# MLP up units: one 512-column matmul for both parts of the activations, and conditioning sums once a layer

## The reference

```python
def sq_relu_mlp(h, w1, w2):                      # w1 1024 x 4096, w2 4096 x 1024, once in each of two layers
    return jnp.square(jax.nn.relu(h @ w1)) @ w2
...
mod = jax.nn.silu(c) @ w_ada + b_ada             # w_ada 1024 x 3072: shift, scale, gate of the last block
shift, scale, gate = jnp.split(mod, 3, axis=-1)
```

## Time and profile before

| | us |
|---|---|
| median of 3 runs | 997.27 |
| lowest, highest | 995.95, 998.62 |
| the profiled execution | 995.88 |
| its span | 994.0 |

### The profile page before, as it was taken

How to read it: one execution, slowest core, us unless ns; L and a number is a source line. 1 busy time by engine, 2 the same in 40 slices (tenths; PEclk the granted TensorE clock), 3 DMA queues, 4 the chain that set the end, 5 groups by cost and what they waited for, 6 DMA issues and landing times. The chain is left out here.

```text
span 994.0 us, 14517 instructions
## 1 busy us (share of the span) xinstructions
PE 971.0 (98%) x6042; PEld 876.7 (88%) x6042; DVE 647.8 (65%) x843; ACT 507.0 (51%) x624; POOL 14.0 (1%) x12
## 2 busy tenths in 40 slices
PE   6999999999999999999999999998999999999997
PEld 5998888889999988988889999987999999988885
DVE  5889936676666668866676766658434777646473
ACT  6734464564434447555664444447344555445533
POOL 0000000000000000000000000000000000002000
PEclk9999999999999999999999999999999999999999
DMA  9834426466777764634466777765655545456611
GB/s 316 302 128 129 169 85 211 149 213 212 242 242 224 249 216 131 209 128 127 149 212 213 258 233 233 248 176 172 229 194 186 170 135 163 170 182 241 197 58 43
DMA packets 122853, 187.37 MB, mean 188 GB/s; under 512 B 5315, under 2 KB 88740, under 8 KB 122788
## 3 DMA queue, kind: packets, MB, share of 16 engines
q1 hardware_dynamic: 122628, 186.17, 56.8%
q10 hardware_dynamic: 160, 0.27, 0.1%
HBM read 185.37 MB, written 1.06 MB: 188 GB/s over the span
## 5 line engine op out<-in xcount | busy, mean ns | idle before, releaser
L1035 DVE TENSOR_TENSOR wl<-raw,wh 128x2048 fp32r<-128x2048 f32 x156 | 356.8, 2290 | 212.3 <-ACT wh L1606 141.3
L1606 ACT CAST wh<-raw 128x2048 fp32r<-128x2048 f32 x156 | 295.8, 1905 | 171.0 <-PE bank L591 166.3
L591 PE MATMUL bank<-hh,wh 128*128 128x256 f32 x1088 | 310.8, 288 | 2.2 <-DVE wl L1035 1.2
L591 PE MATMUL bank<-hl,wh 128*128 128x256 f32 x1088 | 305.8, 283 | 0.0
L591 PE MATMUL bank<-hh,wl 128*128 128x256 f32 x1088 | 305.4, 283 | 0.0
L591 PEld LDWEIGHTS bank<-hh,wh 128*128 128x128 f32 x1088 | 208.8, 193 | 3.2 <-issue 1.5
L591 PEld LDWEIGHTS bank<-hl,wh 128*128 128x128 f32 x1088 | 208.2, 193 | 0.3
L591 PEld LDWEIGHTS bank<-hh,wl 128*128 128x128 f32 x1088 | 207.6, 192 | 0.2 <-DVE wl L1035 0.2
L591 PE MATMUL bank<-wh,yh 128*128 128x512 f32 x416 | 162.8, 391 | 1.8 <-DVE yl L1035 1.8
L591 PE MATMUL bank<-wl,yh 128*128 128x512 f32 x416 | 162.0, 389 | 0.0
L591 PE MATMUL bank<-wh,yl 128*128 128x512 f32 x416 | 161.9, 389 | 0.0
(11 more groups left out here) (181 smaller groups left out, 713.9 us busy)
## 6 DMA issues: line engine op xcount, KB each, us to landing
raw<-in_mlp_w SPq DMA_DIRECT2D x64, 1024.0 KB, 5.6
raw<-in_w_in SPq DMA_DIRECT2D x40, 1024.0 KB, 5.1
raw<-in_ev_w_in SPq DMA_DIRECT2D x20, 1024.0 KB, 5.8
raw<-in_w_ada SPq DMA_DIRECT2D x12, 1024.0 KB, 5.2
raw<-in_od_w_in SPq DMA_DIRECT2D x12, 1024.0 KB, 5.2
raw<-in_ev_w_out SPq DMA_DIRECT2D x6, 1024.0 KB, 5.0
raw<-in_od_w_out SPq DMA_DIRECT2D x4, 1024.0 KB, 4.9
raw<-in_w_o_conv SPq DMA_DIRECT2D x4, 1024.0 KB, 4.9
```

What stands on the lines that cost most here:

```text
L591: return eng.matmul(o, l, r, start=start, stop=stop, skip_group_check=True)
L1035: return eng.tensor_tensor(o, x, y, op)
L1606: eng.copy(part(wh, u), part(raw, u)).then_inc(S["hi"], 1)
```

## The change

Up units become kind W (`w_forward`). The high and the low activations lie in one tensor `h_parts`, and the eight PSUM banks are allocated as four pairs. For each g and k there are two matmuls: the high weight by both activations at once, 512 columns read in two runs of 256, and the low weight by the high activation, 256 columns, added to the first half of the bank. A unit fills two banks; even units take the pair 0 and 1, odd ones the pair 2 and 3. ScalarE copies the second halves to `wf`, VectorE adds the first halves to them and then does the old operation from SBUF to SBUF; ScalarE waits for that (`hid`) before it squares. `hidden_turned` moves to the banks 4 and 5.

The conditioning units no longer appear on TensorE. `mod_rows` writes into six places; after the up unit i=15 TensorE sums all six units of the layer in one go, and VectorE adds the bias once a layer, in the iteration of the output unit i=13.

```diff
-            us.extend(("F", f"mlp_w1_{layer}", 0, 512 * j + UCOLS * i, f"up{layer}", 2 * j + i) for i in range(2))
+            us.extend(("W", f"mlp_w1_{layer}", 0, 512 * j + UCOLS * i, f"up{layer}", 2 * j + i) for i in range(2))
...
+            def w_forward(u):
+
+                w_hi, w_lo, o = slot(wh, u), slot(wl, u), banks[UNITS[u][5] % 2]
+                if UNITS[u][5] % 2 == 0:
+                    for b in range(2):
+                        wait_bank(eng, u, b)
+                elif UNITS[u][5] == 3:
+                    eng.wait_ge(S["x_col"], SECOND[u - 2])
+                else:
+                    wait_evac(eng, next(v for v in range(u - 1, 0, -1) if UNITS[v][4:] == (UNITS[u][4], UNITS[u][5] - 2)))
                 for g in range(2):
-                    m = mm(PS[2][:, 8 + 2 * i + g:9 + 2 * i + g], part[:, g * P:(g + 1) * P], ones[:, :], True, True)
+                    for k in range(KT):
+                        c = slice(g * P, (g + 1) * P)
+                        mm(o[:, g, :].rearrange("p (a t) -> p a t", a=2), w_hi[:, k, c], h_parts[:, :, k, :], k == 0, False)
+                        m = mm(o[:, g, 0:SEQ], w_lo[:, k, c], hh[:, k, :], False, k == KT - 1)
                 m.then_inc(S["used"], 1)
+
+            def mod_sums(layer):
+
+                eng.wait_ge(S["lo_ada"], 6 * (layer + 1))
+                for i in range(6):
+                    part = mod_part(i)
+                    for g in range(2):
+                        m = mm(PS[0][:, 2 * i + g:2 * i + g + 1], part[:, g * P:(g + 1) * P], ones[:, :], True, True)
+                m.then_inc(S["msum"], 1)
...
+                if role in ("up0", "up1") and i == 15:
+                    wait_evac(eng, at(role, 14))
+                    mod_sums(0 if role == "up0" else 1)
...
-                    stt(halves(wf[:, 512 * (i % RING):512 * (i % RING + 1)]), halves(bank(u)[:, :]), 0.0, x_rms(1 if role == "up0" else 3),
-                        ALU.max, ALU.mult).then_inc(S["evac_dve"], 1)
+                    both = banks[i % 2]
+                    hidden = wf[:, 512 * (i % RING):512 * (i % RING + 1)].rearrange("p (g t) -> p g t", g=2)
+                    eng.wait_ge(S["hlow"], 14 * (0 if role == "up0" else 1) + i - 1)
+                    tt(hidden, both[:, :, 0:SEQ], hidden, ALU.add).then_inc(S["evac_dve"], 1)
+                    wait_evac(eng, u)
+                    stt(hidden, hidden, 0.0, x_rms(1 if role == "up0" else 3), ALU.max, ALU.mult).then_inc(S["hid"], 1)
...
+                for layer in range(2):
+                    if u == at(f"out{2 * layer + 1}", 13):
+                        c = slice(12 * layer, 12 * layer + 12)
+                        eng.wait_ge(S["msum"], layer + 1)
+                        tt(mod[:, c], PS[0][:, 0:12], col2[:, R2_BADA + 12 * layer:R2_BADA + 12 * layer + 12],
+                           ALU.add).then_inc(S["mod"], 1)
...
-                    wait_evac(eng, u)
+                    wait_used(eng, u)
+                    if i >= RING:
+                        eng.wait_ge(S["yl_dve"], 16 * layer + i - RING + 1)
+                    eng.copy(wf[:, c].rearrange("p (g t) -> p g t", g=2), banks[i % 2][:, :, SEQ:2 * SEQ]).then_inc(S["hlow"], 1)
+                    eng.wait_ge(S["hid"], 14 * layer + i - 1)
                     act(wf[:, c], wf[:, c], ACT.Square).then_inc(S["sq"], 1)
```

More of the change, by code:

```diff
@@ L11 @@
+import itertools
 from contextlib import ExitStack
@@ L169 @@
 NU = len(UNITS)
-SLABS = {"F": KT, "C": KT, "T": 4, "B": 2}
+SLABS = {"F": KT, "W": KT, "C": KT, "T": 4, "B": 2}
 EVAC = {"hf": "act", "hq": "act", "hi": "act", "rq": "dve", "rk": "dve", "rv": "act", "hgate": "act",
@@ L181 @@
 for _u, (_kind, _, _, _, _role, _i) in enumerate(UNITS):
-    if _kind == "F":
+    if _kind == "W":
+        _count["dve"] += 1
+        EVAC_AT[_u, None] = _count["dve"]
+        if _i % 2 == 0:
+            BEFORE[_u, 0], BEFORE[_u, 1] = _in_bank
+            _in_bank = [(_u, None), (_u, None)]
+    elif _kind == "F":
         BANK_OF[_u] = _next
@@ L198 @@
                 EVAC_AT[_u, _t] = _count[EVAC[_role]]
+USED_AT = list(itertools.accumulate(int(it[0] != "C") for it in UNITS))
 PHASE = {f"out{p}": p for p in range(7)}
@@ L264, in build @@
         x = place("x", (P, TT, D), F32)
-        hh = place("hh", (P, KT, SEQ), F32R)
-        hl = place("hl", (P, KT, SEQ), F32R)
+        h_parts = place("h_parts", (P, 2, KT, SEQ), F32R)
+        hh, hl = h_parts[:, 0, :, :], h_parts[:, 1, :, :]
         y_at = cursor[0]
@@ L307, in build @@
         assert cursor[0] <= nc.sbuf_usable_end, (cursor[0], nc.sbuf_usable_end)
-        PS = [ctx.enter_context(nc.psum_tensor(f"bank{i}", [P, 512], F32)) for i in range(8)]
+        banks = [ctx.enter_context(nc.psum_tensor(f"banks{i}", [P, 2, 512], F32)) for i in range(4)]
+        PS = [banks[i // 2][:, i % 2, :] for i in range(8)]
         scratch_dram = nc.dram_tensor("bias_scratch", (ATT_HEADS, 384), F32, kind="Internal").ap()
@@ L382, in mod_part @@
         def mod_part(i):
-            return view(4096 + UCOLS * (i % 2), UCOLS)
+            return view(4096 + UCOLS * (i % 6), UCOLS)
         ITEM_UNITS = [at("hi", 1) + n for n, c in enumerate((1, 1, 2, 1, 2, 2, 2, 2, 2, 2, 1)) for _ in range(c)]
@@ L454, in hidden_turned @@
         def hidden_turned(i):
-            return PS[(2, 4)[i]][:, :]
+            return PS[4 + i][:, :]
         def turn_gain(p, j):
@@ L486, in wait_used @@
         def wait_used(eng, u):
-            eng.wait_ge(S["used"], u + 1)
+            eng.wait_ge(S["used"], USED_AT[u])
         def split_by(u):
@@ L557, in _ @@
                 if u == at("aq", 1):
-                    eng.wait_ge(S["mod"], 12)
+                    eng.wait_ge(S["mod"], 2)
                     eng.dma_start(gate_dram.rearrange("o (k p) -> p (o k)", p=P), mod[:, 16:24],
@@ L935, in _ @@
                     continue
-                if kind != "C":
-                    eng.wait_ge(S["hi"], SPLIT_OF[u] + 1)
+                if kind == "C":
+                    continue
+                eng.wait_ge(S["hi"], SPLIT_OF[u] + 1)
                 if u not in NORM_AT:
@@ L950, in _ @@
                     t_forward(u)
-                elif kind == "C":
-                    mod_sums(u)
+                elif kind == "W":
+                    w_forward(u)
                 else:
@@ L1053, in mod_rows @@
                 eng.wait_ge(raw_sem[u % RING], 16 * (u // RING + 1))
-                wait_used(eng, u - RING)
                 eng.wait_ge(S["c_act"], 1)
+                if UNITS[u][5] == 6:
+                    eng.wait_ge(S["msum"], 1)
                 w, o = slot(raw, u), mod_part(UNITS[u][5])
@@ L1486, in _ @@
                     eng.wait_ge(S["x_bc"], SECOND[u])
-                    link(tensor(x_row[SECOND[u]], PS[3][:, 0:SEQ]))
+                    tensor(x_row[SECOND[u]], PS[3][:, 0:SEQ]).then_inc(S["x_col"], 1)
+                    eng.wait_ge(S["x_col"], SECOND[u])
                 if role in ("up0", "up1") and i == 3:
@@ L1525, in _ @@
                     hidden_low(0 if UNITS[v][4] == "up0" else 1, UNITS[v][5])
+                for layer in range(2):
[4 more added lines that the diff above has]
+                           ALU.add).then_inc(S["mod"], 1)
+                        if layer == 1:
+                            eng.wait_ge(S["mod"], 2)
+                            link(stt(gs[:, :], mod[:, KT:2 * KT], 1.0, col2[:, R2_NORM:R2_NORM + KT], ALU.add, ALU.mult))
                 if u == at("hf", 1):
```

15 lines of the change are left out of this document (1 added, 14 removed).

## The result

The changed kernel takes 1004.25 us (median of 5 runs, 1000.14 to 1005.46) where the kernel before takes 997.27 (997.27 again over five of its runs). The ratio, estimated from all the runs (the quotient of the two medians is 1.0070), is 1.0054, 95% interval 1.0037 to 1.007: slower, clear of the noise, and above the range's end of 1001.0. The profiled execution took 1004.25 us, its span is 1002.4: 8.4 us more than the span before.

What follows compares the result with a forecast made beforehand. TensorE's matmul issue and few idle places bound the kernel. Pairs -4.9, sums +0.1, starts +3.4 and clock +1.7 gave +0.3 us on 997.27, so 997.6 on the median, range 992.3 to 1001.0.

Steps and rivals of the forecast that it cites:

- The pairs: Up units: a 512- and a 256-column matmul take 0.3472 us instead of 0.360; 24 units save 4.9 us.
- The conditioning sums: One batch of 24 records a layer: removes 5.3 us and adds 5.4 in all, so the move gives nothing.
- The transfer of the gate: On SP, ahead of the `aq` loads, waiting for VectorE's later add: 17 us of cover, nothing to pay.
- The start of a layer: Up to the first output unit: added waits in VectorE's queue cost 1.70 us a layer, +3.4 in all.
- both-bank wait: First up unit (i=2) also waits for the second token tile's evacuation: its start moves +0.60 us.
- The steady chain: Other 12 units of a layer: longer evacuation chain keeps 3.3 us of cover, so nothing is paid.
- one fall in the four places: Two start stalls and two batches of sums: one clock fall to 1.2 GHz, +1.7 us; between none and four.
- the clock falls at nearly every place: Rival: three or four falls in the four places, 1001.0 to 1002.7 us; chance 0.10.
- The split operand: Rival: the up units' two-run input costs as two matmuls, the 4.9 us saving is gone, 1002.5; chance 0.07.
- the hidden start: Rival: the existing 1.06 us stall hides the layer start's new work and the clock holds, 992.5; chance 0.13.
- the evacuation chain: Rival: the chain bounds every steady period, 12 periods lacking about 0.5 us each, 1003; chance 0.03.
- the signs that the prediction named for being wrong: Pair pitch of 0.36 us, stall near 1.1 us, or the clock falling at neither or at all places.

Runs made afterwards that it cites:

- Grouped: Changed kernel with, for each group of 128 hidden columns, the eight 512-column matmuls first, then the eight of 256; 1003.22 us, ratio 1.0065.
- the kernel with the sums alone: Kernel before with its conditioning sums in one batch a layer, up units still three 256-column matmuls; 999.17 us, ratio 1.0024.
- the kernel with the turned states first: Changed kernel with VectorE's low part of the turned hidden states ahead of the row products in its queue; 997.15 us, ratio 0.9992.

## Why the prediction was wrong

**What bounds it**: right. TensorE's issue and its few idle places set the end; no other engine became the bound.

**The pairs**: the mechanism was right, the size was off. In the first two units the pitch is 0.347 as worked out (207.35 to 212.21 in the changed kernel, 14 pairs); in the later ones it is 11.29/32 = 0.3528. The 192 pairs of a layer's twelve steady units bring 1.1 us less each layer, 2.2 in all. The prediction took the sum of two pitches that were each measured in a row of their own kind; no row showed the two sizes in turn, and the only price that it gave the pair a range for was the input in two runs, which costs nothing. Grouped, the pitch is 0.3484. Why the first two units don't show it I can't say. The pairs of output units are 0.03 us longer (10.94 for 10.91), 0.3 in all. Of the 4.9 us, 2.7 arrived.

The Trainium skill ("TensorE: Matmul & The Clock Gate", section Back-to-back issue gap) gives the fixed part of 2.5 ns for an isolated matmul; the prediction had estimated a saving of 1.0 us by it. For the matmuls of this kernel it does not hold: 2.7 us arrived, and the pitches are 0.120 and 0.227 us.

**The conditioning sums**: right. 2.60 us predicted and measured, -2.72 against +2.71 and +2.60 in the kernel with the sums alone. The transfer of the gate cost nothing.

**The start of a layer**: right in every piece. +0.67 for the both-bank wait (0.60), a stall of 2.39 (2.58), +1.75 a layer (1.70).

**The steady chain**: right, nothing is paid. (By its own terms the cover left was 4.9 - 0.59 - 0.69 - 0.4 = 3.2 us less the handshakes, not 3.3.)

**The clock: here it failed.** The step is "I take one fall in the four places". In the profile there were three, one of them twice as long; over all profiles it is six in ten for each kind of place. Four places at 0.6 and 1.7 us are 4.1 us at least, where 1.7 was taken. The reason that I gave for the batches was a near row without a fall, the 32 products at clock 1.00; for the stalls I had one row with a fall and one without and took neither as a count. That row was one toss. The same block in the kernel with the turned states first (its windows and the block itself):

```profile
395.51 4.25 PE L602 MATMUL banks<-wg,work 128*128 128x8 f32 x32
...
398.00:406.00 8.00, 8.00 (x44) 8.00 (x44) 5.81 (x11) 3.39 (x6) 0.00 (x0) 0.57 0.69 240
```

8 x 0.43 = 3.4 us lost, and a distance to the next layer of 128.57 us where it had been 125.54. Eight of the thirteen profiles show it. One execution that shows no fall tells that a fall isn't certain, and nothing more; I had used it as if it told that there is none.

**The rivals.** The one that came is the first, "the clock falls at nearly every place", for which the prediction gave 1001.0 to 1002.7 and a chance of 0.10. The time lies above that rival's own upper end: the pairs brought 2.2 us less, one fall took 3.4, and the profiled start was 0.9 late. The split operand is refuted, the hidden start too (the start was paid in every kernel that kept the order), and the evacuation chain never showed.

**The sum.** Predicted +0.3. Taking the measured pieces: +0.3 + 2.2 (pitch) + 0.3 (output units) + 0.1 (start) + 4.7 (falls, 6.4 for 1.7) + 0.9 (late input) = 8.5, against 8.35. The range ended at 1001.0, which is three falls of 1.7 us with every other term exact (four are the upper end of the rival); it did not add the bounds of the other terms to that case. The lower end of the forecast's own range is a slip as well: 995.9 less the 2.0 of the start is 993.9, not 994.5.

In medians the changed kernel is 7.0 us above before, not 8.4, because the profile of before lies 1.4 us under its median and the changed kernel's lies on its own. The forecast had added these 1.4 us for the changed kernel too.

None of the signs that the prediction named for being wrong showed: the pair takes 0.353 us and not 0.36, the stall is 2.4 and not 1.1, and the clock fell at three places, neither at none nor at all. They asked whether each mechanism was there; what went wrong was how often one of them acts and how large it is.

## What to carry to other kernels

Price a thin stretch on TensorE (idle, or one-column matmuls) twice: its own length, and a fall of the clock behind it with a chance taken from all places of that kind, not from one execution. Keep such work in pieces of under a microsecond between wide matmuls: twelve batches of 0.81 us had no fall behind them, ten of 2.6 us had six. A batch saved nothing by its own count here (2.72 us removed, 2.60 to 2.71 added) and put the clock at risk. When an operation joins an engine's queue, look at what stands between it and the engine that waits: moving one low part ahead of eight row products was worth 1.06 us a layer in the kernel before and 2.56 in the changed one.

## What the runs showed of the hardware

- Matmuls of 512 and 256 columns in turn take 0.3528 us a pair in the steady units; eight and eight of them 0.3484, and 0.2272 + 0.120 = 0.3472 would be the sum.
- A moving operand in two runs of 256 costs the same as one of 512: 11.29 and 11.28 us for 64 matmuls.
- A fall takes 1.7 us of clock, sometimes 3.4, and costs about that where TensorE is the bound (1.6 us twice and 3.2 once in the changed kernel). The one at 426 us costs nothing that shows: the kernel before, with it, needs 125.54 us from the first hand-over to the second layer, the changed kernel, without it, 125.47.
- The three profiles with a fall behind the first layer's batch have none behind the 32 products 40 us later; of the ten others eight have. What decides where a fall comes is open.
